# Second mixer: difference matrices of all heads from turned cumulative sums, maxima by a scan

## The reference, cut to what matters

```python
seg = where(mask, a_cs[..., :, None] - a_cs[..., None, :], -inf)
lmat = exp(seg)
y = einsum('bgls,bgrls,bsgrp->blgrp', cb, lmat, x_c)      # cb = C B^T of the head's group
```

```python
dmat = where(mask, bcum[..., :, None] - bcum[..., None, :] + i_c[..., None, :], -inf)
m_t = maximum(m_inter, max(dmat, axis=-1))
w = exp(dmat - m_t[..., None])
s = einsum('blhd,bshd->bhls', q_c, k_c) * w
den = maximum(abs(sum(s, -1)), exp(-m_t));   h = (s @ v) / den
```

## Time and profile before

| | us |
|---|---|
| median of 3 runs | 1180.61 |
| lowest, highest | 1176.37, 1180.99 |
| the profiled execution, its own time | 1179.55 |
| its span in the trace | 1177.7 |

### The profile page before, as it was taken

The page is one execution under the profiler, slowest core; times in us unless marked ns, Lnnn a source line. Parts: engine busy times, 40 slices in busy tenths (PEclk is TensorE's granted clock), DMA queues, the critical chain, the costliest instruction groups (busy, mean ns, idle before and its releaser), DMA issues.

```text
span 1177.7 us, 15019 instructions
## 1 busy us (share of the span) xinstructions
PE 1066.1 (91%) x5640; PEld 890.0 (76%) x5640; DVE 832.0 (71%) x1073; ACT 630.6 (54%) x734; POOL 107.5 (9%) x132
## 2 busy tenths in 40 slices
PE   6999999999999998677886379999999999999994
PEld 5778999999897887677675367777777777777763
DVE  4755776776676444667774868888888888888864
ACT  4553655545556443344333256666666666666642
POOL 0001000000103442643002000000000000000000
PEclk9999999999999999889898599999999999999997
DMA  9533554565254433222200468999999999999960
GB/s 340 204 107 125 179 192 169 177 215 180 76 171 151 144 116 98 72 72 85 94 12 24 169 223 303 344 351 374 347 356 379 355 343 376 350 355 371 343 232 37
DMA packets 129158, 253.64 MB, mean 215 GB/s; under 512 B 4144, under 2 KB 42160, under 8 KB 129072
## 3 DMA queue, kind: packets, MB, share of 16 engines
q1 hardware_dynamic: 128256, 251.31, 59.7%
q10 hardware_dynamic: 816, 1.23, 0.3%
HBM read 251.47 MB, written 1.05 MB: 214 GB/s over the span
## 4 chain that ended last, share of the span: by engine, by line
PE 77%; DVE 10%; ACT 6%; issue 3%; DMA 3%; POOL 1%; DVEq 0%; POOLq 0%; SPq 0%; ACTq 0%
PE bank L1657 20%; PE bank L1658 20%; PE bank L1659 20%; PE bank L2101 8%; ACT WH L471 3%; DVE WL L879 3%; DMA raw<-in_exp_w_down 2%; DVE CV L1114 1%; PE bank L2056 1%; PE bank L1671 1%; PE bank L1683 1%; PE bank L1663 1%; DMA cn<-in_cn 1%; POOL sm L1598 1%; PE bank L1916 1%
## 5 line engine op out<-in xcount | busy, mean ns | idle before, releaser
L879 DVE TENSOR_TENSOR WL<-raw,WH 128x2048 fp32r<-128x2048 f32 x209 | 475.1, 2297 | 108.8 <-ACT WH L471 105.5
L471 ACT ACTIVATE WH<-raw 128x2048 fp32r<-128x2048 f32 x209 | 398.4, 1914 | 128.7 <-PE bank L1659 89.1
L1657 PE MATMUL bank<-WH,MXH 128*128 128x512 f32 x568 | 226.3, 398 | 3.2 <-DVE MXL L1518 3.2
L1658 PE MATMUL bank<-WL,MXH 128*128 128x512 f32 x568 | 222.8, 392 | 0.0
L1659 PE MATMUL bank<-WH,MXL 128*128 128x512 f32 x568 | 222.6, 392 | 0.0
L1657 PE MATMUL bank<-HTH,WH 128*128 128x256 f32 x576 | 167.9, 291 | 3.0 <-DVE WL L879 1.7
L1658 PE MATMUL bank<-HTL,WH 128*128 128x256 f32 x576 | 165.3, 287 | 0.0
L1659 PE MATMUL bank<-HTH,WL 128*128 128x256 f32 x576 | 165.2, 287 | 0.0
L1657 PEld LDWEIGHTS bank<-WH,MXH 128*128 128x128 f32 x568 | 107.6, 189 | 24.9 <-DVE MXL L1518 3.5
L1657 PE MATMUL bank<-WH,HTH 128*128 128x512 f32 x296 | 119.5, 404 | 6.7 <-DVE HTL L896 3.3
L1659 PEld LDWEIGHTS bank<-WH,MXL 128*128 128x128 f32 x568 | 107.6, 189 | 23.2
(11 more groups left out here) (313 smaller groups left out, 1218.9 us busy)
## 6 DMA issues: line engine op xcount, KB each, us to landing
raw<-in_exp_w_gate SPq DMA_DIRECT2D x52, 1024.0 KB, 8.8
raw<-in_exp_w_up SPq DMA_DIRECT2D x52, 1024.0 KB, 8.9
raw<-in_exp_w_down SPq DMA_DIRECT2D x52, 1024.0 KB, 6.9
raw<-in_w_in SPq DMA_DIRECT2D x34, 1024.0 KB, 5.0
raw<-in_w_up SPq DMA_DIRECT2D x22, 1024.0 KB, 5.3
raw<-in_w_down SPq DMA_DIRECT2D x11, 1024.0 KB, 5.5
raw<-in_w_out SPq DMA_DIRECT2D x8, 1024.0 KB, 5.1
raw<-in_w_o SPq DMA_DIRECT2D x4, 1024.0 KB, 5.5
```

Source lines behind the costliest of these rows:

```text
L471: e.activation(WH[i % HL][:, :], raw[i % RAW][:, :], ACT.Copy).then_inc(a_wh, 1)
L879: e.tensor_tensor(l[:, :], r, h[:, :].bitcast(F32), ALU.subtract).then_inc(v_wl, 1)
L1657: e.matmul(out_, ah, bh, start=start, stop=False)
L1658: e.matmul(out_, ah, bl, start=False, stop=False)
```

## The change

- **Cumulative sums.** The scaled steps `dt*a` of the 16 SSD heads and the log forget gates of the 8 mLSTM heads lie side by side (`AL`, 24 columns per tile). Three float32 matmuls against the triangle and ones give all 24 cumulative sums per token. VectorE copies them (`CS`), negates 16 of them (`csn`), forms input gate minus cumulative sum (`rv`), and splits each into an fp32r value and a remainder (`RW`, 48 columns per tile). PE turns them into rows (48 rows of 256), and ScalarE copies them to `rowsT`.
- **SSD differences.** `ssd_seg` is one fp32r matmul: one-hot weights, a column of `esel` broadcast to 128, pick value and remainder of the head from `rowsT` for all 128 output rows; it writes 256 columns. VectorE adds the per-token negated sum and takes the minimum with 0 in two passes (256 and 128 columns) into `EE`; ScalarE takes the exponential in place. The upper triangle is no longer zeroed by a mask: it is cut by the minimum and by the mask in `CB`.
- **mLSTM differences.** `ml_d` adds an fp32r copy of the -1e30 mask (by the identity) and the picked row of `rv`; the per-token part is left out. The maxima of all heads come from one running-maximum scan over 256 tokens on 8 partitions, turned back by PE and negated (`nmx`); `ml_exp` reads PSUM with this as its bias. `nmt`, with the per-token sum added, stands in `divide`.
- **GpSimd** makes no more masks; it keeps the `XS` product, the powers and a memset.
- **Order.** `small_proj` moves between xbc 4 and xbc 5, to banks 0 and 1. The turn of the rows stands inside `z1` half 0, that of the maxima inside `z1` half 1. On ScalarE three constant copies and the copy to `rowsT` stand ahead of `z_job(1)`. On VectorE the scan stands between the two splits for `v0`. In the SSD loop VectorE does the minimum of head h, and then the product of head h-1; the banks are free once the minimum is done. `ml_max` is gone. `ml_y(h)` waits for the exponential of head h+1, and `columns` of ssd1 for that of head 0.

```diff
 PE
+            for c in range(6):
+                if c == 5:
+                    small_proj(32, 1)
...
+            e.wait_ge(v_lf, 1)
+            e.wait_ge(v_adt, 1)
+            bs = bank[0]
+            e.matmul(bs[:, 0:24], tri, AL[:, 0, :], start=True, stop=True)
+            e.matmul(bs[:, 24:48], ones, AL[:, 0, :], start=True, stop=False)
+            e.matmul(bs[:, 24:48], tri, AL[:, 1, :], start=False, stop=True).then_inc(p_cum, 1)
+            def turn_rows():
+                e.wait_ge(v_cum, V_CUM["rows"])
+                for t in range(T):
+                    ts = slice(t * 128, (t + 1) * 128)
+                    e.transpose(bank[1][0:48, ts], RW[:, t, :], ident)
+                    m = e.transpose(bank[2][0:8, ts], rv[:, t, :], ident)
+                m.then_inc(p_cum, 1)
+            def turn_max():
+                e.wait_ge(v_cum, V_CUM["max"])
+                for t in range(T):
+                    m = e.transpose(bank[3][:, 8 * t:8 * t + 8], cmax[:, t * 128:(t + 1) * 128], ident[0:8, 0:8])
+                m.then_inc(p_cum, 1)
...
             def ssd_seg(h):
-                    e.wait_ge(a_sege, h - 1)
-                e.wait_ge(g_la, h + 1)
-                e.matmul(b[:, 0:256], la[:, 0:128], ux[:, 0:256], start=True, stop=False)
-                e.matmul(b[:, 128:256], la[:, 256:384], ux[:, 0:128], start=False, stop=True)
-                e.matmul(b[:, 256:384], la[:, 128:256], ux[:, 0:128], start=True, stop=True).then_inc(p_seg, 1)
+                    e.wait_ge(v_mn, h - 1)
+                e.matmul(bank[4 + h % 2][:, 0:256], row_of(h), rowsT, start=True, stop=True).then_inc(p_seg, 1)
...
             def ml_d(h):
-                e.wait_ge(g_mr, h + 1)
-                e.matmul(b[:, 0:128], ux[:, 0:128], R[:, 0:128], start=True, stop=True)
-                e.matmul(b[:, 128:256], ux[:, 128:256], R[:, 0:128], start=True, stop=False)
-                e.matmul(b[:, 128:256], ux[:, 0:128], R[:, 256:384], start=False, stop=True)
-                e.matmul(b[:, 256:384], ux[:, 0:128], R[:, 128:256], start=True, stop=True).then_inc(p_mld, 1)
+                e.matmul(b[:, 0:384], ident_r, neg_r, start=True, stop=False)
+                e.matmul(b[:, 0:128], row_of(16 + h), rowsT[:, 0:128], start=False, stop=False)
+                e.matmul(b[:, 128:384], row_of(16 + h), rowsT, start=False, stop=True).then_inc(p_mld, 1)
             def ml_y(h):
-                    e.wait_ge(v_dd, h + 2)
+                    e.wait_ge(a_emx, 2 * h + 4)
 ScalarE
+            e.activation(esel, cn[0:48, CN["esel"]:CN["esel"] + 24], ACT.Copy).then_inc(a_cum, 1)
+            e.activation(ident_r, ident, ACT.Copy).then_inc(a_cum, 1)
+            e.activation(neg_r, const("neg", 384), ACT.Copy).then_inc(a_cum, 1)
+            e.wait_ge(p_cum, P_CUM["turned"])
+            e.activation(rowsT, bank[1][0:48, 0:256], ACT.Copy).then_inc(a_cum, 1)
             z_job(1)
 VectorE
             for h in range(17):
                 if h < 16:
-                    e.wait_ge(a_sege, h + 1)
-                    e.tensor_tensor(EE[h % 3], EE[h % 3], CB[:, h // 8, :], ALU.mult).then_inc(v_ww, 1)
+                    ee, b = EE[h % 3], bank[4 + h % 2]
+                    e.wait_ge(p_seg, h + 1)
+                    if h > 2:
+                        e.wait_ge(p_y, h - 2)
+                    e.tensor_scalar(ee[:, 0:256], b[:, 0:256], csn[:, 0, h:h + 1], 0.0, ALU.add, ALU.min)
+                    e.tensor_scalar(ee[:, 256:384], b[:, 128:256], csn[:, 1, h:h + 1], 0.0, ALU.add,
+                                    ALU.min).then_inc(v_mn, 1)
+                if h:
+                    ee = EE[(h - 1) % 3]
+                    e.wait_ge(a_sege, h)
+                    e.tensor_tensor(ee, ee, CB[:, (h - 1) // 8, :], ALU.mult).then_inc(v_ww, 1)
                 if h % 2 == 0 and h < 16:
                     split(PI[fill[h // 2]] + 2)
+                if h == 2:
+                    e.wait_ge(p_cum, P_CUM["max"])
+                    e.tensor_scalar(nmx, bank[3][:, 0:16].rearrange("p (t c) -> p t c", t=T), -1.0, None,
+                                    ALU.mult).then_inc(own.up(), 1)
+                    e.wait_ge(own.sem, own.n)
+                    e.tensor_tensor(nmt, nmx, CS[:, :, 16:24], ALU.subtract).then_inc(v_cum, 1)
```

More of the change, by code:

```diff
@@ L70, in constants @@
     c[:, CN["ux"]:CN["ux"] + 384] = np.concatenate([tri, np.ones((P, P)), tri], 1)
-    c[:, CN["slt"]:CN["slt"] + 128] = i[:, None] > i[None, :]
+    for h in range(24):
+        for part in range(2):
+            c[(16 * part + h if h < 16 else 16 + 8 * part + h), CN["esel"] + h] = 1.0
     neg = np.where(i[None, :] > i[:, None], NEG, 0.0)
@@ L109 @@
                 for j in range(4 if s in ("mix", "ffn", "n1", "n2") else 2)])
+P_CUM = numbered(["sums", "turned", "max"])
+V_CUM = numbered(["bias", "rows", "max", "nmx"])
+A_CUM = numbered(["sel", "ident", "neg", "rows"])
 RSTD = numbered([(s, t) for s in ("mix", "attn", "ffn", "fin", "n1") for t in range(T)] + ["ssd0", "ssd1"]
@@ L1162, in vector @@
                                 bc(DTv[:, t, :].unsqueeze(2), P, 16, 64), ALU.mult).then_inc(v_xd, 1)
-            for kh in range(2):
-                split(PI["z1", kh] + 2)
+            split(PI["z1", 0] + 2)
+            e.wait_ge(p_cum, P_CUM["turned"])
+            e.tensor_tensor_scan(cmax, bc(ones[0:8, 0:1], 8, 256), bank[2][0:8, 0:256], -3.0e38, ALU.mult,
+                                 ALU.max).then_inc(v_cum, 1)
+            split(PI["z1", 1] + 2)
             def gated(g):
@@ L1200, in vector @@
             group_norm(1)
[L1202 to L1212, removed]
             def ml_sums(h):
@@ L1859, in tensor @@
             warm(8, 0)
-            for c in range(6):
-                k = CVT["xbc", c, 0]
-                feature_tiles(PI["xbc", c], (6, 7) if c % 2 else (4, 5), 0,
-                              ((v_cvt, k - 4), (v_cvt, k - 3)) if c > 1 else (), True, cols=None if c else "n1")
             def small_proj(n, k):
@@ L1870, in small_proj @@
                         col_ready("n2", i)
[L1871 removed]
+                    m = three(bank[SPB[k]][0:n, 0:256], h[:, i, :], l[:, i, :], HTH[:, i, :], HTL[:, i, :], i == 0,
+                              i == 7)
                 m.then_inc(p_sp, 1)
@@ L1997, in tensor @@
             ml_d(0)
-            columns(XS[:, :, 512:1024], (5, 4), ((v_gn, 3), (v_gn, 4)), ((a_sege, 16), (v_dd, 1)))
+            columns(XS[:, :, 512:1024], (5, 4), ((v_gn, 3), (v_gn, 4)), ((v_mn, 16), (a_emx, 2)))
             for h in range(8):
```

141 lines of the change are left out of this document (66 added, 75 removed).

## The result

The changed kernel takes 1182.12 us, median of 17 runs (1179.77 to 1184.71), against 1178.48 us (1176.37 to 1180.99) of the kernel before, 17 runs on the same chip: ratio 1.0032, 95% interval [1.0023, 1.0041]. It is 0.3% slower; within the 0.5% that the prediction calls no change, and 14 us from the 1168 that it forecast (3.6 us more than before by the medians, where 13.0 less was forecast). The profiled execution took 1181.13 us, its span is 1179.3, 1.6 more than before.

What follows compares the result with a forecast made beforehand. PE's summed work was taken to bound the SSD heads, a chain through other engines the mLSTM heads. Terms -0.3 (ahead of the heads), -4.5 (SSD) and -8.2 (mLSTM) sum to -13.0 us, so 1168 us, range 1163 to 1173.

Steps and rivals of the forecast that it cites:

- the mLSTM heads: Second half of the second mixer: earlier `columns`, no `ml_max`, cheaper `ml_d` and some clock sum to -8.2 us, bounds -6 and -10.
- the 1.8, 1.8 and 0.5: Sign to look for in the mLSTM heads: PE's waits ahead of `ml_y` of about these lengths in us.
- rival C: mLSTM heads: stretches at clock 0.86 and 0.93 go near 1.0, three more times 1.5 us, 1163 us; chance 0.13.
- the term for the move of the small projection: Ahead of the SSD heads: with the projection moved, the transposes start near 373.5 instead of 375.3, -1.7 us.
- the stops: SSD heads: at each odd head PE stands 1.44 us before `ssd_y`, waiting for VectorE; the wait for GpSimd goes.
- a pair of heads gains nothing (between -0.15 and +0.15): SSD heads: two short seg and a stop of 1.55 make 1.8 us, where two seg of 0.9 stood.
- after 1.62 us the clock stayed 1.00: Argument against a clock loss behind the new SSD stops, from the wait of that length for L896.
- two new seg of 0.12: SSD heads: each fp32r seg matmul of 256 columns was priced at 0.12 us, where float32 seg took about 0.9.
- the two minimum passes: SSD heads: VectorE's minimum passes of 256 and 128 columns from PSUM take 0.72 us, between 0.63 and 0.83.
- Rival A: SSD heads: low clock pays the gain back, 8 new stops at 1.65 us make 13.2, so 1181 us; chance 0.11.
- Rival B: SSD heads: clock stays low through the fillers, 192 matmuls 0.2 us slower each, 38 us, 1206 us; chance 0.06.
- D: SSD seg: broadcast one-hot weights run at fp32's rate, 0.49 instead of 0.12, 5.9 us back, 1174 us; chance 0.03.

Runs made afterwards that it cites:

- e9: The changed kernel with about 1.6 us of VectorE passes put back ahead of each mLSTM head's row sums: 1187.66 us, ratio 1.0082 to the kernel before.
- e4: The changed kernel with the small projection and ScalarE's copy of it back behind xbc 5: 1184.72 us, ratio 1.0045 to the kernel before.
- e2: The changed kernel with six unused float32 matmuls filling the stop between seg and `ssd_y` at odd heads: 1168.5 us, ratio 0.9905 to the kernel before.
- e3: The kernel before, with `ssd_y` at even index waiting one product longer: 1191.91 us, ratio 1.0103 to the kernel before.
- e5: e3 with one more VectorE pass over 128 columns ahead of the product at odd heads: 1195.66 us, ratio 1.0159 to the kernel before.
- e7: The changed kernel with the previous head's product between the two minimum passes at odd heads: 1176.92 us, ratio 0.9991 to the kernel before.
- e10: e8 with each seg matmul issued twice: 1159.62 us, ratio 0.9846 to the kernel before.
- e1: The changed kernel with VectorE's products done in pairs at even heads, under the fillers: 1161.98 us, ratio 0.9853 to the kernel before.
- e8: e1 with VectorE's `C B^T` mask and the sums ahead of the second weight split for `z1`: 1159.98 us, ratio 0.9847 to the kernel before.

## Why the prediction failed in one step

**Right: the mLSTM heads.** -8.2 was forecast, -8.5 measured. `columns`: -2.1 forecast, 5.7 to 3.4 measured. `ml_max`: -4.6 forecast, 6.8 to 2.1 measured, and e9 gives it back (+5.0 us in this stretch). The single waits are 0.8, 0.8 and 0.4; the 1.8, 1.8 and 0.5 that the prediction lists as a sign do not fit its own -4.6. The waits for the convolution were to stay, and do (12.0 for 11.6). That leaves 1.9 us for `ml_d` and the clock (-1.0 and -0.5 forecast), which no run separates. The granted clock there is 0.84 in both stretches, so rival C did not come.

**Right: ahead of the heads.** The 2.8 us wait in front of the transposes measured 2.6, the first seg starts at 388.60 (388.4 forecast). But the term for the move of the small projection did not show: with the projection back, e4 has the first seg at 388.73.

**Right: the stops.** One in front of `ssd_y` at each odd head, 1.44 us forecast, 1.30 to 1.49 measured, and GpSimd's wait gone. The two numbers are not of one measure: the forecast counts from 0.12 us behind the start of seg, the profile from its end 0.38 behind it. From the start of seg to the start of `ssd_y` 1.56 was forecast and 1.68 came (416.15 to 417.83).

**Wrong: "a pair of heads gains nothing (between -0.15 and +0.15)".** It lost 2.1 us (10.67 for 8.58). Three terms of it failed, and the first is most of it. It is the cost left out behind the stop: "after 1.62 us the clock stayed 1.00" was taken as an answer for stops of 1.4. Measured, the 24 fillers take 1.58 us longer (418.97 to 426.12, where they took 5.57), and e2, where the same order with PE kept busy has no slow filler, shows it to be the clock. Why the inference failed is shown only in part. The wait of 1.62 us stands once, among full work; here the stop stands in every pair, and the same edit had thinned the seg on both sides of it. e3 and e5 show that repetition alone is not enough: the kernel before carries stops of 1.17 us, and most of those of 1.5, without the fall. e7 shows that with short seg even 1.04 us brings it.

The second term is "two new seg of 0.12": 0.12 us is the spacing of such matmuls among their own kind. The seg in front of the fillers costs 0.32, and the last matmul of `ssd_y` in front of each of the two seg 0.32 for 0.22, together +0.4. The third is the two minimum passes, 0.83 for 0.72 (a value from a neighbouring row, within its stated bounds), which makes the +0.12 from seg to `ssd_y`. The sum over the pair is 1.58 + 0.4 + 0.12 = 2.1. Over seven and a half pairs this is about 15.8 of the 16.1 us between -4.5 and +11.6.

Rival A named this mechanism with 8 x 1.65 = 13.2 us and 1181; it was given 0.11. It was right in kind and near in size (1.58 for 1.65 a stop), and it lacks the 0.5 us a pair of the other two terms. The rule of the Trainium skill cited there ("TensorE: Matmul & The Clock Gate", section "A second HAM failure mode: psum-queue depth-cycling") holds here: short repeated idle times made the clock swing, 6 to 12 slow matmuls behind each of seven stops of 1.3 us. It does not hold for every such series: the five first stops of 1.17 us in e3 left the clock at 1.00. Rival B did not come, since the clock recovers within each filler. D did not either: seg at 0.31 us is below the 0.49 of the float32 rate, and a second one costs 0.12 (e10).

**Open.** The number of slow fillers is explained by neither the stop's length nor the work around it alone; the runs give the order in the table, no threshold, and each from one traced execution. What makes the seg slot 0.31 us is open too. That `ml_s(6)` to the end is 1.3 us shorter was not followed up.

## What to carry to other kernels

When an edit shortens PE's work next to a wait, price the clock behind the wait anew: what a wait of the same length did once, in full work, says little about one in every round with less work around it. Before accepting such a stop, look for an order that puts the awaited work under a long run of matmuls: here that was one exchange in VectorE's list, worth 20 us, and it turned the same change from 0.3% slower to 1.5% faster (e1, e8). Take the price of a matmul from a row where it stands between the neighbours that it will have, not from a run of its own kind.

## Not expected of the hardware

- Work added made no time or gave time back: six matmuls in each stop took 13.6 us off (e2). 16 more seg matmuls cost 1.2 us by h=14, and the clock, low at another place, gave it back (e10).
- In e5 PE was busy 33.97 of 40 us at a granted clock of 1.00, in the changed kernel's heads 76.60 of 88.60 at 0.83: the busy share of a stretch does not tell its clock.
- An fp32r matmul of 256 columns between float32 ones of 64 columns: 0.31 us, and 0.10 on the one before; a second of its kind 0.12.
- tensor_scalar with two operations out of PSUM: 483 ns for 256 columns, 342 for 128. The half size costs 71% of the whole.
- The same wait did and did not lower the clock: 2.42 us in front of the turned small projection, 0.86 behind it in the kernel before, 1.00 in e4.
